# DeltaNet output tail of a hybrid encoder layer, moved into a coroutine of its own

## The reference

```
u = rms_norm(x, g1);  proj = u @ w_in
A = rms_norm(chunked band attention over 8 heads of 64, with relative bias)
q, k, v = silu(causal conv of width 4 over proj's delta columns), 4 heads of 128
decay = exp(-exp(A_log) * softplus(a + dt_bias));  beta = sigmoid(b)
per chunk:  v_new = value - k_cumdecay @ S
            o     = q_decay @ S + attn_intra @ v_new
            S     = S * chunk_decay + k_tail^T @ v_new
B = rms_norm(o) * silu(dgate)
h = x + concat[A, B] @ w_out
h = h + relu(rms_norm(h) @ w1)^2 @ w2
```

## Time and profile before

| what | us |
|---|---|
| median of 2 runs | 4742.86 (4741.59 to 4744.13) |
| the profiled execution | 4747.66 |
| its span on the slowest core (core 3) | 4746.1 |
| spans of the eight cores | 4724.1 to 4746.1 |
| DeltaNet stage, up to its last `catdn` | ends at 3113.2 |

### The profile page before, as it was taken

One profiled execution on the slowest core, in us unless ns is written; L12 is line 12 of the kernel. 1 busy time (PEld: TensorE's weight loads), 2 busy tenths in 40 slices (PEclk: granted clock), 3 DMA queues, 4 the chain that ended last, 5 costly groups with the idle time before them and its releaser, 6 DMA issues.

```text
span 4746.1 us, 61221 instructions; the slowest of 8 cores (4724.1 to 4746.1 us)
## 1 busy us (share of the span) xinstructions
PE 2322.5 (49%) x17270; PEld 1710.4 (36%) x17270; DVE 1850.2 (39%) x4422; ACT 1791.0 (38%) x4248; POOL 969.6 (20%) x1763
## 2 busy tenths in 40 slices
PE   1444444444454444534444434314665663187878
PEld 1333333333343343433333333202444442155554
DVE  2555555555455555555555555511112111100000
ACT  3444444444444444444444444323333332212121
POOL 1222222222222222222222222100000000022222
PEclk9666666666666565566666666655666665598989
DMA  2000000000000000000000000040011013500000
GB/s 88 19 10 19 10 10 19 10 19 10 10 19 10 19 10 10 19 10 10 10 10 10 10 10 5 1 124 27 27 36 45 27 39 117 195 23 32 24 30 27
DMA packets 34205, 137.07 MB, mean 29 GB/s; under 512 B 4944, under 2 KB 4944, under 8 KB 30800
## 3 DMA queue, kind: packets, MB, share of 16 engines
q1 hardware_dynamic: 33872, 133.15, 8.5%
HBM read 116.34 MB, written 16.78 MB: 28 GB/s over the span
## 4 chain that ended last, share of the span: by engine, by line
PE 35%; DVE 22%; issue 15%; ACT 14%; DMA 8%; POOL 5%; DVEq 1%; ACTq 1%; SPq 0%; POOLq 0%
PE ps L251 31%; DVE cv L282 7%; ACT cs L261 3%; PE psT L255 3%; DMA xt<-xs 3%; DMA fstg<-w_ff 2%; ACT PTa L261 2%; DVE cv L275 2%; POOL sq L271 2%; DVE Sst L282 2%; DVE XB L271 2%; POOL Kd L271 1%; DVE At L282 1%; DVEq L191 1%; ACT ub L264 1%
## 5 line engine op out<-in xcount | busy, mean ns | idle before, releaser
L251 PE MATMUL ps<-uT,Win 128*128 128x256 bf16 (+1 forms) x3168 | 562.0, 351 | 15.5 <-ACT cv L261 11.7
L282 DVE SCALAR_TENSOR_TENSOR cv<-prw,smallt,cv 128x256 f32<-128x256 f32 x876 | 443.9, 507 | 94.6 <-DVE cv L275 2.3
L251 PE MATMUL ps<-sq,ones_bf 128*128 128x256 bf16 x164 | 61.3, 374 | 853.9 <-POOL sq L271 853.8
L251 PEld LDWEIGHTS ps<-uT,Win 128*128 128x128 bf16 x3168 | 375.4, 128 | 137.3 <-issue 20.7
L271 POOL TENSOR_TENSOR cs<-cv,cs 128x256 f32<-128x256 f32 x292 | 232.8, 797 | 741.9 <-ACT cs L261 650.7
L251 PEld LDWEIGHTS ps<-sq,ones_bf 128*128 128x128 bf16 x164 | 17.5, 107 | 893.4 <-issue 893.4
L255 PE MATMUL psT<-ident_bf,ub 128*128 128x128 bf16 x672 | 132.8, 290 | 412.8 <-DVE uT L289 264.6
L271 POOL TENSOR_TENSOR aT<-rz 128x256 bf16<-128x256 f32 x256 | 156.7, 612 | 569.8 <-ACT rz L261 563.9
L261 ACT ACTIVATE cs<-cv 128x256 f32<-128x256 f32 x292 | 121.7, 417 | 400.2 <-DVE cv L282 370.6
L261 ACT ACTIVATE cs<-cs 128x256 f32<-128x256 f32 x584 | 243.4, 417 | 54.5 <-ACT cs L261 1.5
L251 PE MATMUL ps<-nT,W 128*128 128x256 bf16 x2048 | 245.1, 286 | 5.2 <-ACT nT L261 5.2
(11 more groups left out here) (178 smaller groups left out, 5522.5 us busy)
## 6 DMA issues: line engine op xcount, KB each, us to landing
xt<-xs SPq DMA_DIRECT2D x84, 512.0 KB, 3.7
fstg<-w_ff SPq DMA_DIRECT2D x32, 1024.0 KB, 6.3
stg<-w_in SPq DMA_DIRECT2D x8, 1028.0 KB, 6.0
xres<-xs SPq DMA_DIRECT2D x16, 512.0 KB, 4.4
out<-xres SPq DMA_DIRECT2D x16, 512.0 KB, 2.9
hh<-out SPq DMA_DIRECT2D x16, 512.0 KB, 5.0
out<-obuf SPq DMA_DIRECT2D x16, 512.0 KB, 2.8
stg<-w_in SPq DMA_DIRECT2D x8, 768.0 KB, 5.0
```

What stands on the lines that cost most here:

```text
L251: P.op("pe", lambda e: e.matmul(out, lhsT=lhsT, rhs=rhs, start=start, stop=stop, skip_group_check=skip), r=[lhsT, rhs], w=[out], dur=d_)
L282: P.op("dve", lambda e: e.scalar_tensor_tensor(out=out, in0=in0, scalar=scalar, in1=in1, op0=op0, op1=op1), r=[in0, scalar, in1], w=[out], ...
```

## The change

For own blocks in the DeltaNet stage (`split`) the recurrence no longer computes the output. `O1` is computed at its start, right behind `Rr`, in bank 6. After the new state `S3a` spawns the new coroutine `S3o`, which does `Odn`, the squares, the gate projection, `sg` and `catdn`, all in bank 6, while `S3a` of the next block may run. `Vn`, `O1`, `Odn`, `rec` and `sg` get two buffers each, chosen by the block's parity. Bank 6 is taken out of the rotation of S2 in the whole stage, also in the rounds without own recurrence.

```diff
-            pd_banks = [2, 3, 5, 6] if deep else [2, 3]
+            pd_banks = [2, 3, 5] if deep else [2, 3]
...
+                split = deep and own
+                cpar = blk % 2
+                Vn = Vn_l[cpar] if split else Vn_l[0]
+                O1 = O1_l[cpar] if split else O1_l[0]
...
+                if split:
+                    pO_ = psb[6]
+                    for h in range(4):
+                        mm(pO_[:, h * 128:(h + 1) * 128], dqT[A][h][:, tsl], Sbf[:, h, :])
+                    for h in range(4):
+                        ts("dve", O1[:, h, :], pO_[:, h * 128:(h + 1) * 128], ed[:, h:h + 1], None, ALU.mult)
                 yield
...
-                if own:
+                if own and not split:
...
+                if split:
+                    yield ("spawn", [S3o(blk)])
                     return
...
+            def S3o(blk):
+                sb, tt = divmod(blk, TT)
+                A = sb % NA
+                Bs = blk % NBS
+                c = blk % 2
+                tsl = slice(tt * 128, (tt + 1) * 128)
+                ob = sb - npre
+                Vn, O1, Odn, rec, sg = Vn_l[c], O1_l[c], Odn_l[c], rec_d[c], sg_d[c]
+                pO_ = psb[6]
+                for h in range(4):
+                    mm(pO_[:, h * 128:(h + 1) * 128], PTd[Bs][:, h, :], Vn[:, h, :])
+                tten("dve", Odn[:].rearrange("p h c -> p (h c)"), pO_[:, 0:512], O1[:].rearrange("p h c -> p (h c)"), ALU.add)
+                yield
+                for h in range(4):
+                    act(O1[:, h, :], Odn[:, h, :], AF.Square, accum=rec[:, h:h + 1])
+                rstd_(rec[:, 8:12], rec[:, 0:4], 1.0 / 128, EPS)
+                for kt in range(8):
+                    mm(pO_[:, 0:512], uT[A][:, kt, tsl], Wc(kt, 3072, 3584), start=(kt == 0), stop=(kt == 7))
+                silu_(sg[:], pO_[:, 0:512], sg[:])
+                yield
+                for h in range(4):
+                    stt(catdn[:, ob * TT + tt, h * 128:(h + 1) * 128], Odn[:, h, :], rec[:, 8 + h:9 + h],
+                        sg[:, h * 128:(h + 1) * 128], ALU.mult, ALU.mult)
                 yield
```

More of the change, by code:

```diff
@@ L475, in build_program @@
                 rres = SB(s1, "rres", [128, 4, 128], BF16)
-                Vn = SB(s1, "Vn", [128, 4, 128], BF16)
-                O1 = SB(s1, "O1", [128, 4, 128])
-                Odn = SB(s1, "Odn", [128, 4, 128])
+                NV = 2 if deep else 1
+                Vn_l = [SB(s1, f"VnL{c}", [128, 4, 128], BF16) for c in range(NV)]
+                O1_l = [SB(s1, f"O1{c}", [128, 4, 128]) for c in range(NV)]
+                Odn_l = [SB(s1, f"Odn{c}", [128, 4, 128]) for c in range(NV)]
+                Vn, O1, Odn = Vn_l[0], O1_l[0], Odn_l[0]
             if deep:
-                rec = SB(s1, "rec", [128, 16])
-                sg = SB(s1, "sg", [128, 512])
+                rec_d = [SB(s1, f"rec{c}", [128, 16]) for c in range(2)]
+                sg_d = [SB(s1, f"sg{c}", [128, 512]) for c in range(2)]
             if attph:
@@ L756, in S3a @@
                 if not own:
+                    return
+                if split:
+                    yield ("spawn", [S3o(blk)])
                     return
```

## The result

The changed kernel takes 4782.84 us (median of 15 runs, 4771.81 to 4850.66); the kernel before, run beside it, 4746.03 us (median of 14, 4734.59 to 4823.72). The ratio is 1.0098, with a 95% interval of 1.0063 to 1.0133: about 1% slower. Forecast were 4719 us, within 4668 to 4768, so both the sign and the range were wrong.

A forecast was written before the change was run, and what follows sets the result against it. No engine is full; each round is a chain, with PE waiting for POOL's sq and DVE standing at sg. +7.5 - 24 - 1 - 6 = -23.5 us on the 4742.86 us median gives 4719 us, range 4668 to 4768.

The forecast's parts named there:

- part 2: Own rounds 25 to 30: moving the tail gains 4 us a round, -24 us in all.
- Part 1: One bank fewer for S2: 0.3 us lost in each of 25 rounds without own recurrence, +7.5 us.
- Step 1 gets later: Head of an own round: second block's Rr, O1 and rres delay the last uT copy and projection, +3 us.
- Step 2 gets the second tail: First to second norm matmul: gains Odn, sg1's wait, sg, catdn; loses O1, rres, Vn; +3 us.
- The long step loses everything: Second to third norm matmul (step 3): Odn, Sst, sg's wait, sg and catdn leave, -11.2 us, counted as -10.
- Part 3: The stage's end: round 31 -1 us, last round -6 us (36.4 us instead of 42.3).
- Rival 1: S2's shorter bank rotation decides: strong form +4 us a round, about 4860 us; chance 0.05 strong, 0.07 mild.
- mild form: Bank rotation costs 1.2 us a round, giving 4742 us; chance 0.07.
- Rival 2: Head of own rounds decides: S1's chain starts later, +4 us a round, 4767 us; chance 0.15.
- Rival 3: The split hides sg's waits wholly: own rounds fall to 109 us, 4661 us in all; chance 0.12.
- Rival 4: Tail emitted at once with its sg wait, steps only change places, only the end gains: 4743 us; chance 0.13.
- near 8 us a round instead of 11.3: Sign for the forecast in own rounds: DVE's wait at sg falls to this.

The follow-up runs named there:

- e1: The kernel before with bank 6 taken out of S2's rotation and nothing else; ratio to before 1.0053.
- e2: The changed kernel with bank 6 back, all four banks in one rotation that O1, Odn and the gate share; ratio to before 1.005.
- e13: The changed kernel with only the second block's output coroutine 6 us (model time) later; one run of 4819.34 us, some cores at lower clock; own rounds 119.3 us.
- e14: The changed kernel with only the first block's output coroutine 6 us (model time) later; one run of 4751.17 us, own rounds 119.7 us.
- e4: The changed kernel with four banks and the split in the last superblock only; ratio to before 0.9975.
- e3: The changed kernel with the tail run inside the recurrence's coroutine, O1 still early; one run of 4847.66 us, some cores at lower clock; own rounds 122.9 us.
- e15: The changed kernel with both output coroutines 6 us (model time) later and bank 6 back in the rotation; 4738.82 us, ratio to before 0.997.
- e12: The split kernel with four shared banks, two copies of Sbf and O1 as the spawned tail's first step; 4721.54 us, ratio to before 0.9958.
- e6: The split kernel with four shared banks, O1 back behind Vn, the rest of the tail still spawned; one run of 4731.27 us.
- e8: The split kernel with four shared banks, two copies of Sbf and O1 in the spawned tail, first run; 4724.89 us.

## Why the prediction was wrong

- **The whole.** -23.5 us were forecast (4719 against 4742.86, a ratio of 0.995); the ratio says +46 us (30 to 63), and the profiled execution +33.9 us. Of the 57 us between the forecast's -23.5 and the +33.9 of core 2, part 2 is 45.
- **Part 1, banks: right in kind, low in size.** Taken were 0.3 us for each of 25 rounds, +7.5; it is +13.6 by the medians of the eight cores (+16.0 on core 2; e1: +12.7). I did not have the first round apart: about 3 us there, where S2 has no recurrence beside it. In rounds 1 to 21 it is 0.4 us each, near the walked 0.3, and in rounds 22 to 24 0.8 us each. By its own mark (85.0 to 85.6 us a round for rounds 0 to 21; measured 85.5) part 1 held. Perfetto Trace Analysis of the Trainium skill (section Matmuls) asks for rotation through banks; the measurement agrees, at 0.5% of the time in e1. The price is not the same everywhere: in own rounds a bank fewer costs 0.1 us in e1, at the end of the split kernel 6.0 us (after against e2).
- **Part 2, own rounds: the failed step.** "Step 1 gets later", +3, is +5.1. "Step 2 gets the second tail", +3, is +6.5. "The long step loses everything", -10, is -8.5 and so about right. -4 became +3.0 in round 29 and +3.5 on average, times six. Both wrong terms lie at a wait for sg. I priced the second tail by its DVE operations plus a wait of "about 3 us" for sg1; the wait is 5.43 us, and that is 2.4 of the 3.5 us missing in step 2. In step 1 I saw the last uT copy behind sg0, but walked the projection only 3.7 us later; it is 6.4 us later (39.0 against 32.6), behind an sg0 that waited 6.03 us. And I did not price what stands behind the waiting operation: two of the head's three convolutions stand behind sg1, and behind sg0 the last uT copy, with which the transposes and the projection begin. e13 and e14 show the two places apart, -3.8 and -3.3 us a round.
- **Part 3, the end: the number right, its reason in part.** Last round 36.0 us where 36.4 was worked out, on the path that was walked; round 31 +1.1 where -1 was taken, inside its range. (The marks name 39 us for it; the walk counts from PE's first matmul, from where it is 37.1.) e4 shows the gain alone: 5.9 us. But e3 has the same gain without the overlap of tail and recurrence that the walk is about.
- **Rival 1.** The strong form is excluded by e1; the mild form (1.2 us a round) priced the banks too high in every round but the first.
- **Rival 2 came nearest.** "The head decides" gave +4 us an own round and 4767 us, still 16 us below the median. It had 0.15. Its condition was wrong, though: step 3 shrank by 8.5 us, more than the 6 us named, and the round still lost, since step 2 took back 6.5 of them.
- **Rivals 3 and 4.** 109 us an own round never showed; e15's 116.3 is the least. Rival 3's 109 was also worked out wrong: it adds 2 us to round 24's 107 for DVE's added work, which is 7.5 us by the earlier trace rows. Rival 4's "same three steps" is refuted by the table, although its idea, that the sg wait goes along with the tail, is what happened: 70.2 us for 67.7.
- **What would show it.** Two of the marks told the outcomes apart: "above 122 rival 2" (123.0), and sg's wait "near 8 us a round instead of 11.3", which is 11.5 in round 29.
- **What stays open.** Why e12 spends 117.2 us with its sg between the convolutions and `dqT` while e6, with nearly the same order, spends 118.1 was not tried. Nor is it known why core 2 of e12 starts its first head 1.9 us earlier in round 29 than its seven other cores and e8 do, with the same instructions in the same order. The 2.5 us by which the first norm of e14 is later than before are put down to the second block's `Rr` and `O1` by their place alone; e12, without the early `O1`, has it later too.

## What to carry to other kernels

When an instruction that waits is moved on an in-order engine, price what is queued behind it at its new place, and not the length of its wait: with the same 5.3 to 5.4 us of wait at sg the step was 24.9 us with two convolutions of the critical chain behind it and 19.7 us with none, and moving it to another engine (POOL) only found another link of the chain behind it. Where a small cost model sets the order once for all, a delay of a few microseconds in it is worth trying at two or three values: 0, 6 and 15 us gave 123.0, 116.5 and 122.6 us a round. And take a resource that only some rounds need away from those rounds alone: the bank cost about 14 us in 25 rounds where the output never used it. Last, test each part of a change alone: the end of the stage gained as much without the coroutine (35.3 us in e3) as with it (36.0).

## What the runs showed of the hardware

DVE's fp32 convolution takes longer beside some of POOL's operations. In after's fourth head these rows of DVE

```profile
2907.95 2.42 DVE L282 SCALAR_TENSOR_TENSOR cv<-prw,smallt,cv 128x256 f32<-128x256 f32 x3
2910.29 1.12 DVE L275 TENSOR_SCALAR cv<-prw,smallt 128x256 f32<-128x256 f32 x1
```

fall on these of POOL:

```profile
2909.05 1.04 POOL L271 TENSOR_TENSOR Vb<-Vtm,gsm 128x512 f32<-128x512 bf16 x1
2910.04 1.22 POOL L271 TENSOR_TENSOR Kd<-Ktm,dsm 128x512 bf16<-128x512 bf16 x1
```

The same two kinds take 1.66 us (x3) and 0.34 us in the second head above, so about 1.5 us are lost. It is so throughout the stage (after, core 2, rounds 0 to 30). A convolution's TENSOR_SCALAR takes 345 ns at the median of 246 with nothing on POOL beside it, 816 ns where it starts while POOL's product `cs` is running (17), and 1124 ns beside `Kd` (6). A SCALAR_TENSOR_TENSOR takes 485 ns alone (501) and 760 ns where it starts during the product `cs` (74), but still 485 where it was there first (143), and 1244 ns beside `Vb` (6). POOL pays as well: its product `cs` takes 724 ns alone (94), 889 ns where such a SCALAR_TENSOR_TENSOR was running when it started (143), and 724 ns where it was first itself (39). So the one that starts second takes longer. No run was made for it, and what the two share is not shown here.

This is a rival for the loss of the own rounds: DVE's busy time there grows by 2.3 us. It is not what sets them. e15 has 68.64 us of DVE's work in round 29, 1.3 more than before, in a round that is 3.7 us shorter, and the step from the third head to the fourth, where these rows of after lie, is 17.5 us against 18.1 before. But the place of POOL's `Vb` and `Kd` is one more thing that a new order moves.
